# Attention of a two-block transformer kernel: softmax maps divided on GpSimd and multiplied turned, exponentials one at a time, maps of differential heads combined in pairs, norms read from PSUM

## What is computed

```python
p = jax.nn.softmax(s_own, axis=-1)                      # kind A, causal
y = jnp.einsum('bhqk,bkhd->bqhd', p, v)
p = jax.nn.softmax(s, axis=-1)                          # kind D
a = p[:, :, 0] - lam * p[:, :, 1]
o = jnp.einsum('bhqk,bkhe->bqhe', a, v)                 # then rms norm over 128, gain b_subln
```

## Time and profile before

| | us |
|---|---|
| median of 3 runs (lowest to highest) | 1376.08 (1375.43 to 1377.09) |
| the profiled execution | 1375.88 |
| span of its profile, first to last instruction | 1374.1 |
| around the span | 1.8 |
| PE busy in the span | 1360.0 |
| mean granted clock of PE, 1.0 being full speed | 1.000 |

### The profile page before, as it was taken

How to read it: one execution, slowest core, us unless ns; L and a number is a source line. 1 busy time by engine, 2 the same in 40 slices (tenths; PEclk the granted TensorE clock), 3 DMA queues, 4 the chain that set the end, 5 groups by cost and what they waited for, 6 DMA issues and landing times.

```text
span 1374.1 us, 19191 instructions
## 1 busy us (share of the span) xinstructions
PE 1360.0 (99%) x7393; PEld 1160.3 (84%) x7393; DVE 947.3 (69%) x1192; ACT 712.7 (52%) x941; POOL 126.8 (9%) x141
## 2 busy tenths in 40 slices
PE   9999999999999999999999999999999999999999
PEld 7988888888888888887788888888888877888887
DVE  6894677666677666767666666776667788676665
ACT  5556446444455444576654444544445676544442
POOL 4000003000030000042020000200000331300000
PEclk9999999999999999999999999999999999999999
DMA  9644457655555555553346655565655442565561
GB/s 274 201 161 137 153 182 276 216 190 198 192 166 196 189 183 185 184 182 123 123 154 203 194 183 185 161 206 194 196 189 184 156 152 93 163 204 185 186 198 74
DMA packets 164859, 246.34 MB, mean 179 GB/s; under 512 B 4952, under 2 KB 121860, under 8 KB 164672
## 3 DMA queue, kind: packets, MB, share of 16 engines
q1 hardware_dynamic: 162736, 240.19, 53.6%
q0 software_dynamic: 1776, 4.74, 1.3%
q10 hardware_dynamic: 288, 0.61, 0.1%
HBM read 244.45 MB, written 1.07 MB: 179 GB/s over the span
## 4 chain that ended last, share of the span: by engine, by line
PE 93%; DVE 3%; ACT 3%; issue 1%; POOL 1%; DVEq 0%; ACTq 0%
PE ps L1605 28%; PE ps L1610 15%; PE ps L1572 15%; PE ps L1574 14%; PE ps L1573 14%; PE ps L1859 1%; PE ps L1812 1%; PE ps L1598 1%; DVE wlo L1449 1%; ACT whi L591 1%; PE ps L2111 0%; ACT sc L653 0%; POOL ms L481 0%; ACT pr L653 0%; DVE wlo L939 0%
## 5 line engine op out<-in xcount | busy, mean ns | idle before, releaser
L1605 PE MATMUL ps<-xx,whi 128*128 128x512 f32 x1760 | 422.2, 391 | 0.0
L1605 PEld LDWEIGHTS ps<-xx,whi 128*128 128x128 f32 x1760 | 325.5, 188 | 64.5
L944 DVE TENSOR_TENSOR wlo<-raw,whi 128x2048 fp32r<-128x2048 f32 x120 | 275.1, 2293 | 94.6 <-ACT whi L599 94.6
L599 ACT ACTIVATE whi<-raw 128x2048 fp32r<-128x2048 f32 x120 | 229.6, 1913 | 122.8 <-PE ps L1574 122.4
L591 ACT ACTIVATE whi<-raw 128x2048 fp32r<-128x2048 f32 (+1 forms) x135 | 205.1, 1530 | 84.3 <-PE ps L1574 74.1
L1610 PEld LDWEIGHTS ps<-xx,wlo 128*128 128x128 f32 x1760 | 227.6, 191 | 9.9
L1610 PE MATMUL ps<-xx,wlo 128*128 128x256 f32 x1760 | 230.6, 283 | 0.0
L1572 PE MATMUL ps<-whi,hhi 128*128 128x512 f32 x504 | 198.6, 394 | 0.0
L1573 PE MATMUL ps<-wlo,hhi 128*128 128x512 f32 x504 | 196.8, 390 | 0.0
L1574 PE MATMUL ps<-whi,hlo 128*128 128x512 f32 x504 | 196.3, 389 | 0.0
L939 DVE TENSOR_TENSOR wlo<-raw,whi 128x2048 fp32r<-128x2048 f32 x75 | 171.5, 2288 | 28.4 <-ACT whi L591 28.3
(11 more groups left out here) (276 smaller groups left out, 1374.1 us busy)
## 6 DMA issues: line engine op xcount, KB each, us to landing
raw<-in_ffn_w_gate SPq DMA_DIRECT2D x44, 1024.0 KB, 5.3
raw<-in_ffn_w_up SPq DMA_DIRECT2D x44, 1024.0 KB, 5.3
raw<-in_ffn_w_down SPq DMA_DIRECT2D x44, 1024.0 KB, 5.0
raw<-in_w_in SPq DMA_DIRECT2D x40, 1024.0 KB, 5.2
raw<-in_w_gate_up SPq DMA_DIRECT2D x22, 1024.0 KB, 5.1
raw<-in_w_out SPq DMA_DIRECT2D x12, 1024.0 KB, 5.0
raw<-in_w_down SPq DMA_DIRECT2D x11, 1024.0 KB, 5.0
raw<-in_w_mem_kv SPq DMA_DIRECT2D x4, 1024.0 KB, 5.2
```

Of the source, the lines that this page charges most:

```text
L599: act.activation(whi[:, c % 3, :], raw[:, c % 3, :], ACT.Copy).then_inc(hi_done, 1)
L944: dve.tensor_tensor(wlo[:, c % 3, :], raw[:, c % 3, :], whi[:, c % 3, :], ALU.subtract)\
L1605: return pe.matmul(ps[:, bank + n, :], whi[:, slot, 256 * k + P * n:256 * k + P * n + P], both, start=start, stop=False)
```

## The change

It does these things. (1) First block, kind A: items are ordered by head pair. GpSimd raises the row sums to the power -1 and multiplies the map by them (one pow and two tensor_scalar an item) ahead of the turn, and the product uses the turned form of layer 0, into bank 7. `item_turn(u - 9)` now stands in the middle of unit u (9 to 16), ACT's copy `evac_pT(u - 9)` right behind `hi(u + 3)` in iteration u, and the product still at the end of unit u. ACT copies a finished bank to `hhi` at u = 12 and 16 behind its exponentials, DVE subtracts to `hlo`; DVE's division, the eight transposes at u = 19 and what followed them there are gone. For kind M turn and product change places. (2) Mixers: exponentials stand by item in a table E_AT; for most pairs the second item moves one slot on. (3) Layer 1: `combine` makes one reciprocal and one factor for two items, at slots C_AT, where T_AT of the first item of the pair stands; before it was one slot ahead of T_AT for each. (4) Layer 1: `group_out` stays for the memory heads only. For the others ACT squares and DVE norms read PSUM, and the row sums enter through POOL (EPS times the squared sum). The last group's product goes to bank 3; bank 1 takes the turned second group, and a wait of PE for `y_lo` moves from the turn of item 8 to its product. (5) In the first feed-forward part of the second block (f = 1) the diagonals are made by POOL from one factor and multiplied with the other by ACT, between `up_copy` and `hi(u0 + 4)`.

```diff
-ITEMS = [("A", rt, a, -1) for rt in range(RT) for a in range(AH // 2)]
+ITEMS = [("A", rt, a, -1) for a in range(AH // 2) for rt in range(RT)]
-DIRECT = [layer == 0 for *_, layer in ITEMS]
+DIRECT = [k == "A" or layer == 0 for k, _, _, layer in ITEMS]
+E_AT = ((26, 27, 31, 32, 36, 37, 41, 42, 44, 45, 47, 48, 49, 50, 52, 53),
+        (26, 27, 30, 31, 34, 35, 38, 39, 42, 43, 45, 46, 49, 49, 51, 51))
+C_AT = (28, 32, None, None, 44, 47, 50, 52)
-Y_BANKS = (7, 0, 2, 0)
+Y_BANKS = (7, 1, 2, 0)
+O_BANKS = (1, 1, 1, 3)
...
@@ POOL: row_scale @@
-                    if n == N_F1:
-                        c = place(N_FIN, r)
-                        pool.tensor_scalar(rdg[:, r, :], ident, scale[:, r:r + 1], rstd[:, c:c + 1], ALU.mult, ALU.mult)\
-                            .then_inc(diag_ready, 1)
...
@@ POOL: sub_norm @@
+                pool.tensor_tensor(gms[:, j, :], s0, s0, ALU.mult).then_inc(sub_ms, 1)
+                pool.tensor_scalar(gms[:, j, :], gms[:, j, :], EPS, None, ALU.mult).then_inc(sub_ms, 1)
...
+                pool.tensor_tensor(gms[:, j, :], gms[:, j, :], gss[:, j, :], ALU.add).then_inc(sub_ms, 1)
...
+            for i in range(8):
+                nk = P * (ITEMS[i][1] + 1)
+                total = sums[:, 2 * i:2 * i + 2]
+                pool.wait_ge(p_ready, SOFT[i])
+                pool.tensor_tensor(total, total, mone[:, :].to_broadcast([P, 2]), ALU.pow).then_inc(inv_ready, 1)
+                pool.wait_ge(inv_ready, i + 1)
+                for e in range(2):
+                    v = maps(i)[:, SEQ * e:SEQ * e + nk]
+                    ins = pool.tensor_scalar(v, v, total[:, e:e + 1], None, ALU.mult)
+                ins.then_inc(pn_ready, 1)
...
@@ ACT: ffn @@
-                hi(u0 + 4, (u0 + 4) % 3)
+                if f != 1:
+                    hi(u0 + 4, (u0 + 4) % 3)
+                else:
+                    act.wait_ge(fin_diag, 2)
+                    for r in range(RT):
+                        c = place(N_F1, r)
+                        act.wait_ge(rstd_ready, c + 1)
+                        act.activation(rdg[:, r, :], rdg[:, r, :], ACT.Copy, scale=rstd[:, c:c + 1]).then_inc(diag_ready, 1)
+                    hi(u0 + 4, (u0 + 4) % 3)
...
@@ ACT: first block @@
                 if u < PROJ - 1:
                     hi(u + 3, u % 3)
+                if 2 <= u - 7 <= 9:
+                    evac_pT(u - 9)
...
-                    if 1 <= k <= 12:
+                    if 9 <= k <= 12:
                         evac_pT(k - 1)
                     if k < 8:
                         exps(k)
+                    if k in (5, 9):
+                        b = (k - 5) // 4
+                        act.wait_ge(pv_ready, 4 * b + 4)
+                        act.activation(hhi[:, b, :], ps[:, 7, :], ACT.Copy).then_inc(xhi_done, 2)
...
@@ ACT: mixers @@
-                    for i in items_at(S_AT[L], h - 1):
+                    for i in items_at(E_AT[L], h):
                         exps(i0 + i)
...
@@ DVE: mixers @@
-                        for i in items_at(T_AT[1], h + 1):
-                            combine(i0 + i)
+                        for n in items_at(C_AT, h):
+                            combine(i0 + 2 * n)
...
@@ PE: narrow and wide units; item_turn after the first half @@
+                    if n == 0 and turned is not None:
+                        item_turn(turned)
...
@@ PE: item_turn and item_pv @@
-                if L == 1 and i - IT0[L] == 8:
-                    pe.wait_ge(y_lo, 4 * L + 2)
...
-                            pe.wait_ge(o_copied, g)
+                            pe.wait_ge(sc_read, IT0[L] + 16)
...
+                turned = u - 9 if 9 <= u <= 16 else None
...
                     if k < 12:
                         item_scores(k)
-                    if 1 <= k <= 12:
-                        item_turn(k - 1)
                     if 2 <= k <= 13:
                         item_pv(k - 2)
-                if u == 19:
-                    pe.wait_ge(sc_read, 12)
-                    pe.wait_ge(o_evac, 2)
-                    turn_part(T_Y0, 0, xn)
-                    turn_part(T_Y0, 1, xn)
+                    if 9 <= k <= 12:
+                        item_turn(k - 1)
```

More of the change, by code:

```diff
@@ L559, in _ @@
                     norm(N_FIN)
+                    for r in range(RT):
+                        pool.wait_ge(rstd_ready, place(N_FIN, r) + 1)
+                        pool.tensor_scalar(rdg[:, r, :], ident, rstd[:, place(N_FIN, r):place(N_FIN, r) + 1], None, ALU.mult)\
+                            .then_inc(fin_diag, 1)
                     norm(N_F1)
@@ L624, in turned_gain @@
                     if c % 4 < 2:
-                        act.wait_ge(tr_ps, 4 * T + 2 * half + c % 2 + 1)
+                        act.wait_ge(tr_ps, turns_of(T) + 2 * half + c % 2 + 1)
                     else:
@@ L1098, in combine @@
             def combine(i):
[L1100 to L1112 removed]
+                nk = P * (ITEMS[i][1] + 1)
+                s0, s1 = [sums[:, 2 * i:2 * i + 4].rearrange("p (j e) -> p j e", e=2)[:, :, e] for e in range(2)]
+                inv, factor = [rec[:, 32 + 4 * (i // 2 % 2) + 2 * n:34 + 4 * (i // 2 % 2) + 2 * n] for n in range(2)]
+                dve.wait_ge(p_ready, SOFT[i + 1])
+                link(dve.reciprocal(inv, s1))
+                link(dve.scalar_tensor_tensor(out=factor, in0=s0, scalar=lam[:, 4:5], in1=inv, op0=ALU.mult, op1=ALU.mult))
+                for n in range(2):
+                    j = i + n
+                    dve.wait_ge(pT_ready, j - 1)
+                    dve.scalar_tensor_tensor(out=comb[:, j % 2, 0:nk], in0=maps(j)[:, 256:256 + nk],
+                                             scalar=factor[:, n:n + 1], in1=maps(j)[:, 0:nk], op0=ALU.mult, op1=ALU.add)\
+                        .then_inc(comb_ready, 1)
             def ffn(f, u0, follow):
@@ L1339, in _ @@
                         lo(u + 3)
-                    if k == 12:
-                        for b in range(2):
-                            dve.wait_ge(xhi_done, KC * T_Y0 + 2 * b + 2)
-                            dve.tensor_tensor(hlo[:, b, :], ps[:, TURN_BANKS[T_Y0][b], :], hhi[:, b, :], ALU.subtract)\
-                                .then_inc(xlo_done, 2)
                     if 2 <= k < 6:
@@ L1548, in _ @@
                         scores(i0 + i)
-                    if L == 1 and h in V_AT[1]:
-                        i = items_at(V_AT[1], h)[-1]
-                        if i % 4 == 3:
-                            group_out(i // 4)
+                    if L == 1 and h == V_AT[1][7]:
+                        memory_out()
                     if L == 1 and (h - 1) // 8 in (1, 3, 4) and (h - 1) % 8 in (5, 7):
@@ L1645, in row_scales, with narrow @@
                 ins.then_inc(rb_ps, 1)
-            def narrow(u, slot, bank, T=None):
+            def narrow(u, slot, bank, T=None, turned=None):
                 pe.wait_ge(lo_done, u + 1)
@@ L1655, in narrow, with wide @@
                                     k == 0, k == KC - 1)
+                    if n == 0 and turned is not None:
+                        item_turn(turned)
                 ins.then_inc(unit_used, 1)
-            def wide(u, half, banks, free):
+            def wide(u, half, banks, free, turned=None):
                 pe.wait_ge(lo_done, u + 1)
@@ L1666, in wide @@
                                     half == 0 and k == 0, half == 1 and k == 3)
+                    if r == 0 and turned is not None:
+                        item_turn(turned)
                 ins.then_inc(unit_used, 1)
@@ L1856, in item_pv @@
                         else:
[L1857 removed]
+                            v = z1[:, b, 3, size * h:size * h + size]
                         c = P * (e * nb + b)
@@ L1918, in _ @@
                         pe.wait_ge(*free(tiles))
-                    narrow(u, u % 3, tiles % 4)
+                    narrow(u, u % 3, tiles % 4, turned=turned)
                     tiles += 1
@@ L1924, in _ @@
                     else:
-                        wide(u, u % 2, (tiles % 4, (tiles + 1) % 4), (free(tiles), free(tiles + 1)))
+                        wide(u, u % 2, (tiles % 4, (tiles + 1) % 4), (free(tiles), free(tiles + 1)),
+                             turned)
                     tiles += 2 * (u % 2)
```

109 lines of the change are left out of this document (52 added, 57 removed).

## The result

| | before | after |
|---|---|---|
| median of 6 runs each | 1376.10 us | 1400.26 us (1395.34 to 1402.18) |
| the profiled execution | 1375.88 | 1398.47 |
| its span | 1374.1 | 1396.7 |
| mean granted clock of PE | 1.000 | 0.991 |

The changed kernel takes 1.0169 times as long as the kernel before over all runs, with a 95% interval of 1.016 to 1.0179; the two medians alone give 1.0176. The forecast was 1386.5 us and the range ended at 1395, so the sign and the place were right and the size was not.

The account below looks back on a forecast made before the run. PE, busy 1360.0 of 1374.1 us, was taken as the bound. First block +13.1, layer 0 -2.2, layer 1 -1.0 and diagonals +0.4 summed to +10.3 us, hence 1386.5 us; range 1381 to 1393, with rivals 1380 to 1395.

Parts of the forecast that it names:

- The gaps: First block, units 9 to 16: PE waits for ACT's copy behind the split; gaps 22.9 us, first block +13.1 us.
- The mid-unit turns and the cheaper product: First block: 24 transposes inside units cost 3.1 us; turned product 1.2 us cheaper, already counted in the gap.
- GpSimd: First block's division on POOL: 2.9 to 6 us an item against about 10 us available, so not waited for.
- Rival A: First block: GpSimd late, turn waits for its division; +9 to +18 us, to 1395 to 1405 us; chance 0.12.
- Layer 0: Second block's layer 0 mixer: moving second items' exponentials one slot on removes waits of 0.97, 0.43 and 0.77 us; -2.2 us.
- Layer 1: Second block's layer 1 mixer: later paired combines cost, other waits shrink; sum -1.0 us, bounds -5.7 and +3.
- The diagonals: At f = 1: wait for GpSimd goes (-0.7), queue behind ACT's products costs +1.1; +0.4 us, bounds -0.7 and +3.
- Rival C: First block: copy not behind the split, about -2 us; with -3 from the mixers, 1371 us; chance 0.03.

Follow-up runs that it names:

- e2: Changed kernel plus 14 idle transposes of the identity ahead of each of the eight turned kind A products; 1388.67 us.
- e12: Changed kernel plus 7 idle transposes ahead of each of the eight turned kind A products; 1389.38 us.
- e1: Changed kernel with ACT's copy of the turned map issued ahead of the weight split, not behind it; 1374.42 us.
- e3: Kernel before, with only the changed kernel's first-block places of turn, copy and product; VectorE still divides, mixers as before; 1404.7 us.
- e6: e4's kernel with both items' exponentials of a pair in the same slot again in layer 0; 1373.43 us against 1371.34.
- e7: e4's kernel with the f = 1 diagonals made by GpSimd from both factors again, without ACT's products; 1371.91 us against 1371.34.
- e4: e1's kernel with layer 1's maps combined one item at a time, one slot ahead of each turn, as in the kernel before; 1371.34 us.
- e9: Kernel with copy first, single combines and later sigmoid (1369.50 us), with layer 1's turns of items 2 and 3 one slot later; 1373.46 us.
- e11: e1's kernel with the copy behind the split again in unit 12 only; 1377.30 us.

## Why the prediction was right and wrong

- **The gaps.** Right in kind: eight waits for ACT's copy, right behind each split. Measured from the first score to the next dense matmul the eight gaps are 3.43, 3.20, 2.77, 3.31, 2.90, 3.20, 2.86 and 3.63 us, 25.3 in all, where the prediction had 22.9. e2 and e12 give 14.7 to 14.8 us for the waiting against its +13.1.
- **The step that failed.** The prediction counted every wait of PE as its own length and no more; it read the clock as 1.00 in the kernel before and left it there. The new waits were to be 1.2 to 1.9 us and were 1.84 to 2.25, longer than any wait of the earlier trace rows, and six of them had some 3 us at 1.2 GHz behind them. That term, 9 to 10 us, is most of the miss; the waiting, 1.7 us more than forecast, is the rest: 13.1 + 1.7 + 9.2 = 24.0. e2 removes the clock's part without touching the waits' cause, e1 with it.
- **The mid-unit turns and the cheaper product.** Not measured one by one. With the waits gone (e1) the first block is 0.3 us from the kernel before without the start-up, two waits of 1.8 us included.
- **GpSimd.** That it would not be waited for was right. Its price was too high: the prediction's own terms (0.7 for the pow, twice 0.6 to 1.1, and none or one blocked start of 2.3) make 1.9 to 5.2 us an item, not 2.9 to 6, and the items take 1.9 (0.72 + 1.19) to 4.1 us (0.72 + 3.42). Rival A falls: PE waits for GpSimd nowhere in the first block, and e3 has the loss without it. VectorE's split lasts 2.29 us beside GpSimd's work as without it, so in the rows seen here it is GpSimd that is held, and not the split. This agrees with the rule of the Trainium skill that the prediction weighed (SBUF — State Buffer, "Who interferes with whom") in that one engine is held, and bears out the choice not to follow it to a late turn.
- **Layer 0.** -2.2 forecast, -2.4 measured, and e6 undoes it with the table alone.
- **Layer 1.** The waits were well placed: 2.75 us for the first pair over two blocks (forecast "about 2.8"), none at slot 44. The sum came out at +1.8 and not -1.0, because 1.7 us of low clock stand behind the 2.75, again the missing term, and because the pairs at slots 28 and 52 wait 0.66 and 0.67 us where +0.3 was taken for each. That is 2.4 of the 2.8 us; the rest is open.
- **The diagonals.** -0.8 against +0.4: the term of +1.1 for the queue behind ACT's products does not show. What made the wait of before go isn't settled, since e7 lost it without those products.
- **Rival C** gave 1371 us if the copy were not behind the split. e1 makes just that change and gives 1374.4, with layer 1's 3.8 us of loss left in; e4 without them 1371.3. That this is C's number is partly luck: C had -2 for the first block and -3 for the mixers, and e4's trace has +0.3 (without the start-up), -0.8 at the diagonals, -2.4 in layer 0 and -2.0 in layer 1.

## What to carry to other kernels

Before moving a consumer next to its producer, read which instruction stands between them on the third engine, and what that instruction waits for: here a copy of 0.4 us inherited a 1.9 us split that could not start before the unit's end. Price a new wait of TensorE twice, once by its length and once by what the clock may do behind it; if no wait in the trace of before is as long as the new one, the trace can't vouch for a clock of 1.00, and even a shorter wait is no surety (e9). And let a place in an order have its own table: an operation whose place follows another's moves with it.

## What the runs showed of the hardware that was not expected

- Waits of about 2 us were enough to bring TensorE from 2.4 to 1.2 GHz for some 3 us, even a single one (e11), and in e3, behind the wait of 1.99 us at 118.13, for twice as long: the granted clock from 118 to 126 is 0.57, a loss of 0.43 x 8 = 3.4 us. Length alone doesn't decide it: in the changed kernel the waits of 1.99 us at 87.57 and 128.36 have a clock of 1.00 behind them, the one of 1.84 us at 96.48 has 0.84. The wait of 2.75 us in layer 1 has 0.83 behind it in the changed kernel and in e1, and 1.00 in e11. The one of 1.29 us in e9 has 0.83, while behind the eight of 0.93 to 1.35 us in e12 the clock stays at 1.00. The six runs of the changed kernel go from 1395.34 us at a mean clock of 0.994 to 1402.18 at 0.989. What tells these waits apart is open.
- Idle transposes in a wait made the kernel 11.6 us faster by the medians (e2).
- A GpSimd instruction of 0.30 us on one column took 2.84 us beside VectorE's splits. Whether it slips in ahead of one shifts GpSimd's chain by 2 us from one kernel to the next (e7), so a wait at the end of such a chain is no fixed price.
